# A context of 256 tokens is loaded in 32 by 32 blocks and turned by VectorE instead of TensorE

## Chip, core and metric

One core of one Trainium2 chip runs the whole kernel in one launch. The metric is the device time in microseconds (us) of that core. The median of three runs before the change is 1671.52 us (1669.97 to 1673.87).

## What is computed

Two blocks follow one another. The first one is two layers of attention (windowed heads and low-rank heads) on 256 tokens of 2048 features. The second one is two mixers on the same tokens, the first of which also needs states made from a context of 256 tokens. All of it is f32. What matters here is how the context enters:

```
# ctx: (1, 256, 2048); sh_c, sc_c come from a modulation of c_ctx, one value a feature
sh_c, sc_c = modulation(c_c, w_ada[i], b_ada[i], 2)
uc = ctx_s * (1.0 + sc_c) + sh_c
s_f, s_b = context_states(uc @ w_in_e[j][:, :E_STATE_COLS], w_gate_f[j], ...)
y, _, _ = even_mixer(u @ w_in_e[j], s_f, s_b, ...)
```

## The kernel before

All weights come from DRAM as one stream of 504 blocks ("slots") of 128 partitions by 1024 values, 512 KB each. SyncE issues them into a ring of 4 tiles `stage` (`load_slot`, line 636); the load of slot n waits until VectorE has split slot n-4. Each slot is split into a high and a low part, since TensorE multiplies in the rounded type fp32r: ScalarE copies `stage` to `wh` (`split_hi`, line 313, called as `hi()`), VectorE subtracts to get `wl` (`split_lo`, line 335, called as `lo()`). These parts have a ring of 4 of their own: `hi()` of slot n waits until TensorE is done with slot n-4. TensorE then does 12 products of 512 columns for the slot (`slot`, lines 396, 397 and 403). Each of ScalarE, VectorE and TensorE runs an order written out by hand, in which other work stands between slots at a fixed slot count n; nothing is planned by a program.

The activations must lie with features on the partitions (`xth` high part, `xtl` low part, 16 feature tiles of 256 tokens). For that, tiles with tokens on the partitions are turned in "turns": a turn is four transpositions of 128 by 128 on TensorE into one of two PSUM banks `TP` (`turn_in`, line 527), then ScalarE and VectorE read the bank (`turn_hi`, line 540, `turn_lo`, line 558). All turns are numbered in `TURNS`, and the bank of a turn is free once its reader has counted it.

The context goes this way in eight turns ("x", 2, m), m = 0 to 7. At the end of the second attention layer ScalarE issues one DMA of 2 MB into `arena` (line 964), when the last head is done. In the layer's last 16 slots, which are the second half of its output projection (named OUTB+0 to OUTB+15 here), TensorE does turns 0 to 3 after slots 6, 10, 14 and 15. The other four stand in front of the first four of the 32 slots of the context's own projection ("context slots"; lines 2470 to 2482). For each turn ScalarE multiplies and adds the modulation columns (`mcols`) in two instructions out of PSUM into the tile `Tb` in SBUF (line 548) and rounds it into `xth` (line 556), and VectorE makes `xtl` (line 568). Context slot m waits for turn m.

Beside this VectorE adds up the modulation of the second block (`mod_op`, line 696, on 512 KB blocks that GpSimd loads, three in flight), at most one instruction a slot, and adds the output projection to `X` (`evac_add`, line 1494). In the context slots, at n = 10, both engines take the statistics of the first block's last norm (`stats_act_sum`, `stats_act_root`, `stats_dve`, lines 614 to 631), at n = 11 and 12 VectorE scales `X` (line 1656), and from n = 28 the latent tokens are turned for the next projections (turn by turn, line 2482, with VectorE's part in line 1677).

Of the kernel before, what the change touches and what calls it, by code (L numbers as in the profile page):

```python
# [13 lines left out]
F32 = mybir.dt.float32  # L14
# [5 lines left out]
P = 128  # L20
# [61 lines left out]
    return t + [("m", l, 1, 1, 0), ("m", l, 1, 1, 1), ("x", l + 1, 2), ("x", l + 1, 3)]  # L82


TURNS = [t for l in range(DEPTH) for t in layer_turns(l)] + [("x", DEPTH, m) for m in range(4, 8)]
TURN = {name: n + 1 for n, name in enumerate(TURNS)}
HIGHS = [t for t in TURNS if t[0] in ("x", "lat", "ya", "yb")]
HIGH = {name: n + 1 for n, name in enumerate(HIGHS)}
# [31 lines left out]
def build(nc, A, out):  # L120
    ctx = ExitStack()
    with ctx:
# [447 lines left out]
        def kts(x, a, n=2):  # L570

            return x[:, a:a + n, :]
# [73 lines left out]
        def weight_of(p):  # L646
# [9 lines left out]
            half, g, m = (p - OUTA) // 16, (p - OUTA) % 16 // 4, p % 4  # L656
            return OUTA + 8 * g + 4 * half + m

        @block.sync
        def _(sp):  # L660
            x = A["x"][0].rearrange("(t p) n -> p t n", p=P)
            for l in range(DEPTH):
                for p in range(N_LAYER):
                    if l == 0 and p == 0:
                        sp.dma_start(X[:, :, 0:256], x[:, :, 0:256]).then_inc(once("x_first"), 16)
                    if l == 0 and 1 <= p < 5:
                        cs = slice(256 if p == 1 else COLS * (p - 1), COLS * p)
                        sp.dma_start(X[:, :, cs], x[:, :, cs]).then_inc(x_loaded[p - 1], 16)
                    if p == 16:
                        sp.wait_ge(st_sum, 2 * l + 1)  # L670
                        sp.dma_start(tail, A["w_tail"][l, :, :]).then_inc(tail_full, 16)
                    n = N_LAYER * l + p
                    load_slot(sp, n, N_LAYER * l + weight_of(p), n % SLOTS)
            with sp.Fori(R_BLOCK1, R_LAT0) as r:
                load_round(sp, r, r)
            with sp.Fori(R_LAT0, R_ODD0) as r:
                load_round(sp, r - R_KV, r)
            load_round(sp, R_ODD0 - R_KV + ODD_ORDER[0], R_ODD0)
            with sp.Fori(R_ODD0 + 1, R_ODD0 + 5) as r:
                load_round(sp, r - R_KV - 1, r)  # L680
            with sp.Fori(R_ODD0 + 5, R_END) as r:
                load_round(sp, r - R_KV, r)
            o = out[0].rearrange("(t p) n -> p t n", p=P)
            for i, (t, a, w) in enumerate(OUT_PIECES):
                sp.wait_ge(once("out_ready"), i + 1)
                sp.dma_start(o[:, t, a:a + w], X[:, t, a:a + w]).then_inc(out_done, 16)
            sp.wait_ge(out_done, 16 * len(OUT_PIECES))
# [100 lines left out]
        def _(act):  # L788
# [19 lines left out]
            def turn(name, dst, scale=None, bias=None):  # L808
                turn_hi(act, link, TURN[name], dst, scale, bias)

            def turn_x(l, m):
                if l < DEPTH:
                    turn(("x", l, m), kts(xth, 2 * m), [gcols[:, l, 2 * m + j:2 * m + j + 1] for j in range(2)])
                    return
                if m in (0, 4):
                    act.wait_ge(mod_cols, 4 if m == 0 else 8)
                turn(("x", l, m), kts(xth, 2 * m), [mcols[:, 0, KT + 2 * m + j:KT + 2 * m + j + 1] for j in range(2)],
                     [mcols[:, 0, 2 * m + j:2 * m + j + 1] for j in range(2)])

            def attention_layer(l):  # L820
                N0, G0, H0, e0 = N_LAYER * l, G_LAYER * l, HEADS * l, 2 * l
# [136 lines left out]
                for n in range(18):  # L958
                    hi()
                    if n == 0:  # L960
                        turn(("yb", l, 3), kts(xth, 14))
                    if n == 2 and l == DEPTH - 1:
                        act.wait_ge(o_done, HEADS * DEPTH)
                        act.dma_start(ar(8192, TT, D), A["ctx"][0].rearrange("(t p) n -> p t n", p=P))\
                            .then_inc(once("ctx_loaded"), 16)
                        act.dma_start(pa[:, 1024:1536], A["w_r"]).then_inc(once("wr_loaded"), 16)
                    if n in (8, 12, 16, 17):
                        turn_x(l + 1, (8, 12, 16, 17).index(n))

            for l in range(DEPTH):  # L970
                attention_layer(l)
# [390 lines left out]
        def _(dve):  # L1362
# [13 lines left out]
                turn_lo(dve, TURN[name], HIGH[name], hi, low, scaled, scale)  # L1376

            def turn_x(l, m):
                scale = [gcols[:, l, 2 * m + j:2 * m + j + 1] for j in range(2)] if l < DEPTH else None
                turn(("x", l, m), kts(xth, 2 * m), kts(xtl, 2 * m), l == DEPTH, scale)  # L1380

            def turn_lat(l, i):
                a, n = LAT_KT[i]
# [18 lines left out]
            def attention_layer(l):  # L1402
# [193 lines left out]
                for n in range(18):  # L1596
                    lo()
                    if n == 0:
                        turn(("yb", l, 3), kts(xth, 14), kts(xtl, 14), False)
                    if n in (8, 12, 16, 17):  # L1600
                        turn_x(l + 1, (8, 12, 16, 17).index(n))
                    if n in (10, 14):
                        mod_unit(1, (n - 10) // 4)
                    if n in (5, 9, 13, 17):
                        evac_add(1, (n - 5) // 4)
                    if n < 5:
                        mod()
# [38 lines left out]

            for n in range(4, 36):
                if n < 8:
                    turn_x(DEPTH, n)
                if n == 10:  # L1650
                    stats_dve(dve, e, [(0, 2, D)], ss, rstd, EPS)
                if n in (11, 12):
                    t = n - 11
                    dve.wait_ge(st_rs, e + 1)
                    dve.wait_ge(once("row_loaded"), 16)
                    nc.vector.scalar_tensor_tensor(out=X[:, t, :], in0=X[:, t, :], scalar=rstd[:, t:t + 1],
                                                   in1=ar(12288, D), op0=ALU.mult, op1=ALU.mult)\
                        .then_inc(once("x_final"), 1)
                lo()
                if n == 12:  # L1660
                    dve.wait_ge(once("wr_hi"), 1)
                    nc.vector.tensor_tensor(wr[:, :, 32:64], pa[:, 1024:1536].rearrange("p (a b) -> p a b", a=KT),
                                            wr[:, :, 0:32].bitcast(F32), ALU.subtract).then_inc(once("wr_ready"), 1)
                    for a in (0, P):
                        nc.vector.tensor_copy(rt_split[96:GK, a:a + P], ones[96:GK, :])
                if n == 23:
                    low_rank_sum(1)
                if n == 28:
                    gates_to_rows(1)
                if 24 <= n < 28:  # L1670
                    c = n - 24
                    dve.wait_ge(once("gate_hi"), c + 1)
                    low = gate_split[c][64:97, :]
                    nc.vector.tensor_tensor(low, gate_full[64:97, 512 * c:512 * c + 512], low.bitcast(F32), ALU.subtract)\
                        .then_inc(once("gate_lo"), 1)
                if n >= 28:
                    turn_scaled(n - 28)
                mod_ctx(n - 4)
# [501 lines left out]
        def _(pe):  # L2180
# [27 lines left out]
                    last = nc.tensor.matmul(AB[1][:, 392 + j:393 + j], macc[:, 0, P * j:P * j + P], ones[:, 0:1], start=True, stop=True)  # L2208
                last.then_inc(mod_summed, 1)

            ctx_tile = ar(8192, TT, D)
            Y = PROJ[:, :, 2048:4096]

            def turn(name, srcs):
# [5 lines left out]
            def turn_x(l, m):  # L2220
                if l == 0:
                    pe.wait_ge(x_loaded[m // 2] if m else once("x_first"), 16)
                elif l == DEPTH:
                    pe.wait_ge(once("ctx_loaded"), 16)
                else:
                    pe.wait_ge(psum_free, G_LAYER * (l - 1) + G_OUTB + m // 2 + 1 + 2)
                turn_rows(("x", l, m), ctx_tile if l == DEPTH else X, 2 * m)

            def attention_layer(l):
                N0, G0, H0 = N_LAYER * l, G_LAYER * l, HEADS * l  # L2230
# [201 lines left out]
                for n in range(16):  # L2432
                    step(OUTB + n)
                    if n == 0:
                        pe.wait_ge(o_done, H0 + HEADS)
                        turn_rows(("yb", l, 3), Y, 14)
                    if n in (8, 12):
                        turn_unit(1, (n - 8) // 4)
                    if n in (6, 10, 14, 15):
                        turn_x(l + 1, (6, 10, 14, 15).index(n))  # L2440
            for l in range(DEPTH):
                attention_layer(l)
# [26 lines left out]

            for p in range(4 * SLOTS):  # L2470
                g, m = p // SLOTS, p % SLOTS
                if p < 4:
                    turn_x(DEPTH, 4 + p)
                if g == 0:
                    turned(pe, TURN["x", DEPTH, m])
                slot(pe, 8 * R_CTX0 + p, G_BLOCK1 + g, KPB * m, m == 0)
                if p == 15:
                    low_rank(1)
                if g == 3:
                    if m == 0:  # L2480
                        pe.wait_ge(once("x_final"), 2)
                    transposes(pe, u, [lambda t, kt=2 * m + j: X[:, t, kt * P:kt * P + P] for j in range(2)])
# [360 lines left out]
```

## Time and profile before

| | us |
|---|---|
| median of three runs | 1671.52 |
| lowest, highest | 1669.97, 1673.87 |
| the profiled execution | 1672.03 |
| its span, first to last instruction | 1670.2 |
| TensorE busy in it | 1643.7 |
| VectorE busy | 1343.9 |
| ScalarE busy | 899.7 |
| DMA, mean over the span | 233 GB/s |

TensorE is busy for 98% of the span, at a mean granted clock of 0.997. All times of day below count from the start of the span. The second attention layer ends and the context slots begin at about 706 us.

### The profile page before, as it was taken

The numbers are of one execution on the slowest core, as the hardware profiler recorded it, in microseconds if no ns is written. First come the engines' busy times: TensorE is split into PE (matmuls) and PEld (weight loads), VectorE is DVE, ScalarE is ACT, GpSimd is POOL, SyncE is SP. The second block draws the span as 40 slices with busy tenths as digits, with TensorE's granted clock in tenths as the row PEclk, the third lists the DMA queues.
The fourth block names the chain that finished last, engine by engine and source line by source line (L and its number), as shares of the span: only waits on it lengthen the run. The fifth ranks groups of instructions, "written<-read, shape, count | busy, mean of one in ns | idle before, by whom it ended". The sixth has DMA issues, their size and how long they took to land.

```text
span 1670.2 us, 23384 instructions
## 1 busy us (share of the span) xinstructions
PE 1643.7 (98%) x8638; PEld 1400.1 (84%) x8638; DVE 1343.9 (80%) x1772; ACT 899.7 (54%) x1348; POOL 157.4 (9%) x221
## 2 busy tenths in 40 slices
PE   9999999999999999999999999999999999999996
PEld 8888888888888888887877878888877879999985
DVE  6998778979987878787985788888876988867766
ACT  6447564445466654565853466666534374445532
POOL 1100000001100000011211110010101101110000
PEclk9999999999999999999999999999999999999998
DMA  9975555658855545789987964345859869887663
GB/s 328 323 251 176 176 166 164 207 193 292 289 172 173 187 145 182 270 284 331 358 282 235 295 226 136 130 138 182 317 185 341 311 217 293 275 269 261 240 203 111
DMA packets 113160, 388.86 MB, mean 233 GB/s; under 512 B 18252, under 2 KB 19164, under 8 KB 111676
## 3 DMA queue, kind: packets, MB, share of 16 engines
q1 hardware_dynamic: 74944, 268.99, 45.9%
q0 software_dynamic: 27824, 101.18, 19.8%
q10 hardware_dynamic: 10286, 17.25, 3.0%
q8 instruction: 69, 1.13, 0.3%
q14 instruction: 37, 0.30, 0.1%
HBM read 383.19 MB, written 4.19 MB: 232 GB/s over the span
## 4 chain that ended last, share of the span: by engine, by line
PE 93%; DVE 3%; DMA 2%; ACT 1%; issue 1%; DVEq 0%; ACTq 0%; SPq 0%
PE L L396 22%; PE L L397 22%; PE L L403 22%; PE L L442 4%; PE L L438 4%; PE L L436 4%; PE TP L534 3%; PE AB L2601 2%; PE AB L2301 1%; DMA stage<-in_w_stream 1%; PE TP L2314 1%; PE AB L2535 1%; PE AB L2617 1%; PE AB L2304 1%; PE AB L2327 1%
## 5 line engine op out<-in xcount | busy, mean ns | idle before, releaser
L317 ACT ACTIVATE wh<-stage 128x1024 fp32r<-128x1024 f32 x504 | 530.4, 1057 | 463.8 <-PE L L403 221.9
L338 DVE TENSOR_TENSOR wl<-stage,wh 128x1024 fp32r<-128x1024 f32 x504 | 612.8, 1221 | 203.3 <-ACT wh L317 201.8
L396 PE MATMUL L<-wh,xth 128*128 128x512 f32 (+1 forms) x1692 | 680.9, 402 | 1.9 <-DVE xtl L2026 1.3
L397 PE MATMUL L<-wh,xtl 128*128 128x512 f32 (+1 forms) x1692 | 659.0, 389 | 0.0
L403 PE MATMUL L<-wl,xth 128*128 128x512 f32 (+1 forms) x1692 | 454.0, 389 | 0.0
L396 PEld LDWEIGHTS L<-wh,xth 128*128 128x128 f32 x1692 | 318.2, 188 | 67.1 <-issue 3.2
L403 PEld LDWEIGHTS L<-wl,xth 128*128 128x128 f32 x1692 | 317.5, 188 | 66.4 <-DVE wl L338 1.0
L397 PEld LDWEIGHTS L<-wh,xtl 128*128 128x128 f32 x1692 | 318.5, 188 | 62.7 <-issue 2.4
L714 DVE SCALAR_TENSOR_TENSOR macc<-mstage,scols,macc 128x1024 f32<-128x1024 f32 x240 | 306.8, 1278 | 4.3 <-DMA mstage<-in_w_mod 3.8
L781 POOL DMA_DIRECT2D mstage<-in_w_mod x192 | 138.9, 724 | 1240.7 <-DVE macc L714 1044.5
L436 PE MATMUL L<-xth,wh 128*128 128x256 f32 x512 | 125.8, 284 | 0.0
L438 PE MATMUL L<-xtl,wh 128*128 128x256 f32 x512 | 125.6, 283 | 0.0
L438 PEld LDWEIGHTS L<-xtl,wh 128*128 128x128 f32 x512 | 98.4, 192 | 0.0
L436 PEld LDWEIGHTS L<-xth,wh 128*128 128x128 f32 x512 | 98.3, 192 | 0.0
L854 ACT ACTIVATE pa<-pa,st 128x128 f32<-128x128 f32 x96 | 43.0, 449 | 68.4 <-DVE st L1464 37.9
L442 PE MATMUL L<-xth,wl 128*128 128x256 f32 x512 | 71.9, 283 | 0.0
L442 PEld LDWEIGHTS L<-xth,wl 128*128 128x128 f32 x512 | 66.1, 192 | 0.0
L866 ACT ACTIVATE pa<-TP 128x384 f32<-128x384 f32 x48 | 23.5, 490 | 62.4 <-PE TP L2314 62.3
L534 PE MATMUL TP<-ident,arena 128*128 128x128 f32 x288 | 41.1, 273 | 3.7 <-ACT arena L980 2.3
L534 PEld LDWEIGHTS TP<-ident,arena 128*128 128x128 f32 x288 | 34.2, 141 | 10.9 <-issue 3.0
L1141 ACT ACTIVATE arena<-arena 128x256 f32<-128x256 f32 (+1 forms) x84 | 34.1, 464 | 16.8 <-DVE arena L1806 16.8
L1458 DVE SCALAR_TENSOR_TENSOR pa<-tab,AB 128x384 f32<-128x384 f32 x48 | 26.5, 552 | 19.3 <-PE AB L2305 16.3
(275 smaller groups left out, 1464.5 us busy)
## 6 DMA issues: line engine op xcount, KB each, us to landing
stage<-in_w_stream SPq DMA_DIRECT2D x504, 512.0 KB, 4.6
mstage<-in_w_mod POOLq DMA_DIRECT2D x192, 512.0 KB, 6.2
arena<-in_ctx ACTq DMA_DIRECT2D x1, 2048.0 KB, 9.2
x_kept<-X ACTq DMA_DIRECT2D x4, 512.0 KB, 10.3
X<-x_kept ACTq DMA_DIRECT2D x1, 2048.0 KB, 8.3
arena<-in_b_ada ACTq DMA_DIRECT2D x2, 1024.0 KB, 9.1
arena<-in_ln_g ACTq DMA_DIRECT2D x2, 1024.0 KB, 8.8
X<-in_x SPq DMA_DIRECT2D x3, 512.0 KB, 8.1
```

The costliest lines, as they stand in the source:

```text
L317: nc.scalar.activation(wh[:, s % SPLITS].rearrange("p a b -> p (a b)"), stage[:, s % RING, :], ACT.Copy).then_inc(hi_ready, 1)
L338: nc.vector.tensor_tensor(wl[:, s % SPLITS].rearrange("p a b -> p (a b)"), stage[:, s % RING, :], wh[:, s % SPLITS].rearrange("p a b -> p ...
L396: nc.tensor.matmul(dst[:, t, 0:width], xh, w, start=start and k == 0, stop=False, skip_group_check=True)
L397: nc.tensor.matmul(dst[:, t, 0:width], xl, w, start=False, stop=False, skip_group_check=True)
L403: last = nc.tensor.matmul(dst[:, t, 0:width], x[0][:, kt + k, t * P:t * P + P], wl[:, slot, k, 0:width], start=False, stop=True, skip_grou ...
L436: nc.tensor.matmul(o[:, j, :], w, xth[:, kt + k, :], start=start and k == 0 and j % 2 == 0, stop=False, skip_group_check=True)
L438: nc.tensor.matmul(o[:, j, :], w, xtl[:, kt + k, :], start=False, stop=False, skip_group_check=True)
L442: last = nc.tensor.matmul(o[:, j, :], wl[:, s, k, P * j:P * j + P], xth[:, kt + k, :], start=False, stop=True, skip_group_check=True)
L534: last = nc.tensor.transpose(bank[0:width, j, t * P:t * P + P], src(t), ident[:])
L714: nc.vector.scalar_tensor_tensor(out=acc, in0=block, scalar=col, in1=acc, op0=ALU.mult, op1=ALU.add).then_inc(mod_sum, 1)
L781: pool.dma_start(mstage[:, unit % MOD_UNITS, :].rearrange("p (c n) -> p c n", c=2), WM[n // KPB, :, 2 * cp:2 * cp + 2, COLS * k:COLS * k + ...
L854: ins = nc.scalar.activation(pr[b][:, a:a + w], pr[b][:, a:a + w], ACT.Exp, bias=ngm[:, 2 * b + t:2 * b + t + 1], scale=1.0 if swa else ML ...
```

## The change

The context comes into SBUF already cut in blocks of 32 by 32, so that what is left is a transposition inside each block, which VectorE can do. `ctx_rows(sp, b)` issues four DMAs for 32 tokens: the DMA for a puts columns 32a to 32a+31 of every feature tile on partitions 32a to 32a+31, where the partition is the token within its 32. One such DMA moves 64 KB in 512 pieces of 128 bytes. SyncE issues them behind the loads of slots OUTB+6 to OUTB+13, four after each, 32 in all; ScalarE's DMA of 2 MB goes away.

VectorE's `exchange_ctx(m)` turns the blocks of two feature tiles (128 by 512 values) into `Tb`; ScalarE then modulates in place, out of SBUF and not out of PSUM, and rounds; VectorE's `ctx_low(m)` makes the low part as before. The eight turns on TensorE, and their places in `TURNS`, are gone; context slot m waits for `ctx_low`. On ScalarE the first four come at n = 14, 15, 16, 17 of the layer's last 18 slots (before: 8, 12, 16, 17). On VectorE the exchange of m runs ahead of its low part: exchanges 0 and 1 at n = 14, then one exchange and one low part a slot.

```diff
+        ctx_blocks = ar(8192, KT, TOK)
+        def ctx_rows(sp, b):
+            sp.wait_ge(o_done, HEADS * DEPTH)
+            rows = A["ctx"][0, 32 * b:32 * b + 32, :].rearrange("j (k a i) -> a j k i", a=4, i=32)
+            for a in range(4):
+                sp.dma_start(ctx_blocks[32 * a:32 * a + 32, :, 32 * b:32 * b + 32], rows[a]).then_inc(once("ctx_loaded"), 16)
...
                     load_slot(sp, n, N_LAYER * l + weight_of(p), n % SLOTS)
+                    if l == DEPTH - 1 and OUTB + 6 <= p < OUTB + 14:
+                        ctx_rows(sp, p - OUTB - 6)
...
-                turn(("x", l, m), kts(xth, 2 * m), [mcols[:, 0, KT + 2 * m + j:KT + 2 * m + j + 1] for j in range(2)],
-                     [mcols[:, 0, 2 * m + j:2 * m + j + 1] for j in range(2)])
+                T = Tb[m % 2]
+                act.wait_ge(once("ctx_turned"), m + 1)
+                for j in range(2):
+                    kt = 2 * m + j
+                    ins = nc.scalar.activation(T[:, j, :], T[:, j, :], ACT.Identity, scale=mcols[:, 0, KT + kt:KT + kt + 1],
+                                               bias=mcols[:, 0, kt:kt + 1])
+                link(ins)
+                nc.scalar.activation(kts(xth, 2 * m), T, ACT.Copy).then_inc(once("ctx_high"), 1)
...
-                        act.dma_start(ar(8192, TT, D), A["ctx"][0].rearrange("(t p) n -> p t n", p=P))\
-                            .then_inc(once("ctx_loaded"), 16)
...
+            def exchange_ctx(m):
+                if m == 0:
+                    dve.wait_ge(once("ctx_loaded"), 16 * 32)
+                if m >= 2:
+                    dve.wait_ge(once("ctx_low"), m - 1)
+                nc.vector.transpose(Tb[m % 2].rearrange("p a b -> p (a b)"),
+                                    kts(ctx_blocks, 2 * m).rearrange("p a b -> p (a b)")).then_inc(once("ctx_turned"), 1)
+            def ctx_low(m):
+                dve.wait_ge(once("ctx_high"), m + 1)
+                nc.vector.tensor_tensor(kts(xtl, 2 * m), Tb[m % 2], kts(xth, 2 * m).bitcast(F32), ALU.subtract)\
+                    .then_inc(once("ctx_low"), 1)
...
+                    if l == DEPTH - 1 and n >= 14:
+                        if n == 14:
+                            exchange_ctx(0)
+                            exchange_ctx(1)
+                        else:
+                            ctx_low(n - 15)
+                            exchange_ctx(n - 13)
...
                 if n < 8:
-                    turn_x(DEPTH, n)
+                    if n == 4:
+                        ctx_low(3)
+                    if n < 7:
+                        exchange_ctx(n + 1)
+                    ctx_low(n)
...
-                if p < 4:
-                    turn_x(DEPTH, 4 + p)
                 if g == 0:
-                    turned(pe, TURN["x", DEPTH, m])
+                    pe.wait_ge(once("ctx_low"), m + 1)
```

## Rows read from the trace of the kernel before

**Rows 1.** The page's part 1: busy us (share of the span) xinstructions.

```profile
PE 1643.7 (98%) x8638; PEld 1400.1 (84%) x8638; DVE 1343.9 (80%) x1772; ACT 899.7 (54%) x1348; POOL 157.4 (9%) x221
```

**Rows 2.** Waits of TensorE over the span: us in total, times, longest.

```profile
PE TP L534 <- DVE xtl L568: 5.0, 3, 3.5
```

**Rows 3.** Chain of waits, 640 to 830 us, TensorE's part: start us, us, what.

```profile
674.58 0.91 PE L L403 x4
...
692.74 0.91 PE L L403 x4
695.46 0.91 PE L L403 x4
...
701.80 0.92 PE L L403 x4
702.71 0.44 PE TP L534 x4
705.00 0.91 PE L L403 x4
...
708.79 0.91 PE L L403 x4
...
711.99 0.92 PE L L403 x4
```

**Rows 4.** The same chain, 735 to 791 us.

```profile
735.73 1.07 ACT wh L317
...
750.81 8.99 DMA stage<-in_w_stream
...
762.31 13.56 DMA stage<-in_w_stream
...
789.65 0.70 DVE xtl L568
790.40 0.66 PE TP L534 x4
```

**Rows 5.** VectorE's groups by line, 685 to 730 us: busy us, mean ns.

```profile
L338 DVE TENSOR_TENSOR wl<-stage,wh 128x1024 fp32r<-128x1024 f32 x14 | 17.2, 1225 | 9.0 <-ACT wh L317 8.9
L714 DVE SCALAR_TENSOR_TENSOR macc<-mstage,scols,macc 128x1024 f32<-128x1024 f32 x4 | 5.1, 1278 | 0.0
L568 DVE TENSOR_TENSOR xtl<-pa,xth 128x512 fp32r<-128x512 f32 x7 | 4.8, 689 | 1.3 <-ACT xth L556 1.3
...
L711 DVE TENSOR_SCALAR macc<-mstage,scols 128x1024 f32<-128x1024 f32 x1 | 0.7, 748 | 0.0
```

**Rows 6.** VectorE in order of time, 728 to 765 us.

```profile
731.24 0.17 DVE L631 RECIPROCAL st<-st 128x2 f32<-128x2 f32 x1 [1.34 <-ACT st L623]
732.19 1.23 DVE L338 TENSOR_TENSOR wl<-stage,wh 128x1024 fp32r<-128x1024 f32 x1 [0.78 <-ACT wh L317]
```

**Rows 7.** Stretches: us; PE, PEld, DVE, ACT, POOL busy; PEclk, DMA share, GB/s.

```profile
665.00:670.00 5.00, 5.00 (x24) 4.14 (x23) 5.00 (x5) 0.76 (x1) 0.82 (x2) 1.00 1.00 415
...
663.00:685.00 22.00, 22.00 (x104) 18.30 (x104) 19.81 (x21) 11.00 (x13) 2.17 (x3) 1.00 0.99 378
...
690.00:710.00 20.00, 20.00 (x103) 16.49 (x103) 12.77 (x17) 12.11 (x18) 0.00 (x0) 1.00 0.54 172
...
1366.50:1367.00 0.50, 0.50 (x3) 0.39 (x3) 0.10 (x1) 0.50 (x2) 0.00 (x0) 1.00 0.56 4
1367.00:1367.50 0.50, 0.50 (x4) 0.36 (x3) 0.00 (x0) 0.50 (x2) 0.00 (x0) 1.00 0.96 7
1367.50:1368.00 0.50, 0.50 (x6) 0.50 (x5) 0.00 (x0) 0.50 (x1) 0.00 (x0) 1.00 0.53 4
```

**Rows 8.** ScalarE's two DMAs of 4-byte pieces, line 1095: issue ns, start, landing.

```profile
L1095 ACTq DMA_DIRECT2D lcols<-in_ln_b x1: 2280/2280/2280, 920.4 to 920.4; - x1
...
DMA to landing us min/median/max: 5.8/6.9/8.0
```

**Rows 9.** ScalarE in order of time, 655 to 740 us.

```profile
671.92 1.06 ACT L317 ACTIVATE wh<-stage 128x1024 fp32r<-128x1024 f32 x1 [6.16 <-DMA stage<-in_w_stream]
```

More of the change, by code:

```diff
@@ L82, in layer_turns @@
     return t + [("m", l, 1, 1, 0), ("m", l, 1, 1, 1), ("x", l + 1, 2), ("x", l + 1, 3)]
-TURNS = [t for l in range(DEPTH) for t in layer_turns(l)] + [("x", DEPTH, m) for m in range(4, 8)]
+TURNS = [t for l in range(DEPTH) for t in layer_turns(l) if t[0:2] != ("x", DEPTH)]
 TURN = {name: n + 1 for n, name in enumerate(TURNS)}
@@ L963, in attention_layer @@
                         act.wait_ge(o_done, HEADS * DEPTH)
-                        act.dma_start(ar(8192, TT, D), A["ctx"][0].rearrange("(t p) n -> p t n", p=P))\
-                            .then_inc(once("ctx_loaded"), 16)
                         act.dma_start(pa[:, 1024:1536], A["w_r"]).then_inc(once("wr_loaded"), 16)
-                    if n in (8, 12, 16, 17):
-                        turn_x(l + 1, (8, 12, 16, 17).index(n))
+                    places = (14, 15, 16, 17) if l == DEPTH - 1 else (8, 12, 16, 17)
+                    if n in places:
+                        turn_x(l + 1, places.index(n))
             for l in range(DEPTH):
@@ L1378, in turn_x @@
             def turn_x(l, m):
-                scale = [gcols[:, l, 2 * m + j:2 * m + j + 1] for j in range(2)] if l < DEPTH else None
-                turn(("x", l, m), kts(xth, 2 * m), kts(xtl, 2 * m), l == DEPTH, scale)
+                turn(("x", l, m), kts(xth, 2 * m), kts(xtl, 2 * m), False, [gcols[:, l, 2 * m + j:2 * m + j + 1] for j in range(2)])
+            def exchange_ctx(m):
[9 more added lines that the diff above has]
+                    .then_inc(once("ctx_low"), 1)
             def turn_lat(l, i):
@@ L1599, in attention_layer @@
                         turn(("yb", l, 3), kts(xth, 14), kts(xtl, 14), False)
-                    if n in (8, 12, 16, 17):
+                    if l < DEPTH - 1 and n in (8, 12, 16, 17):
                         turn_x(l + 1, (8, 12, 16, 17).index(n))
+                    if l == DEPTH - 1 and n >= 14:
[5 more added lines that the diff above has]
+                            exchange_ctx(n - 13)
                     if n in (10, 14):
@@ L2209, in odd_columns @@
                 last.then_inc(mod_summed, 1)
-            ctx_tile = ar(8192, TT, D)
             Y = PROJ[:, :, 2048:4096]
@@ L2222, in turn_x @@
                     pe.wait_ge(x_loaded[m // 2] if m else once("x_first"), 16)
-                elif l == DEPTH:
-                    pe.wait_ge(once("ctx_loaded"), 16)
                 else:
                     pe.wait_ge(psum_free, G_LAYER * (l - 1) + G_OUTB + m // 2 + 1 + 2)
-                turn_rows(("x", l, m), ctx_tile if l == DEPTH else X, 2 * m)
+                turn_rows(("x", l, m), X, 2 * m)
             def attention_layer(l):
@@ L2438, in attention_layer @@
                         turn_unit(1, (n - 8) // 4)
-                    if n in (6, 10, 14, 15):
+                    if l < DEPTH - 1 and n in (6, 10, 14, 15):
                         turn_x(l + 1, (6, 10, 14, 15).index(n))
```

## The prediction

> **What bounds the kernel now.** I read the busy times first: TensorE is busy for 98% of the span, VectorE for 80% [rows 1]. Then TensorE's waits: it waits little, and its longest waits are for VectorE's low part of a turn, 5.0 us in three, one of them 3.5 us [rows 2]. Then I followed the chain of waits through the stretch that the change touches. Up to about 735 us it is TensorE alone, slot after slot: products, turns, products [rows 3]. There the reader should see that a turn costs its own time on the path. Behind that it changes: from 735.73 to 790.40 us the chain goes through ScalarE, VectorE, two weight transfers of 8.99 and 13.56 us and VectorE again, and it gets back to TensorE at 790.40, at a transposition that has waited 3.5 us [rows 2, 4]. So the eight turns are on the path locally, while a barrier some 75 us later is set by VectorE and the DMA queues. What the change brings is what arrives at that barrier, not what TensorE saves in front of it.
>
> **What TensorE saves.** The low products of two slots with nothing between them start 2.72 us apart (692.74 and 695.46). With one turn between it is 3.20 us (701.80 to 705.00, 708.79 to 711.99), although the turn's own piece is 0.44: the next slot begins more slowly. With two turns, m = 3 and 4, it is 3.79 us (705.00 to 708.79) [rows 3]. So one turn is 0.48 and the pair 1.07; six single ones and the pair make 6 x 0.48 + 1.07 = 3.95 us. All of it falls before 718 us. TensorE also gets new waits, for `ctx_low`; they are walked through below.
>
> **What VectorE pays.** Eight transpositions of 128 by 512 are added; the subtractions stay. The trace has no transposition on VectorE. The nearest rows: a two-input subtraction of 128 by 512 is 0.69 us, one of 128 by 1024 is 1.23, a one-input TENSOR_SCALAR of 128 by 1024 is 0.75 [rows 5]. From below half of the last is 0.37; from above I put twice the 0.69, about 1.3, in case a block is filled and emptied one after the other. I take 0.69, of which the next instruction overlaps about 0.08 (neighbours in time start that much before the end), so 0.61 each and 4.9 us in all. The Trainium skill, "Vector Engine (DVE) Microarchitecture Reference", in what it says of the transpose mode, has it pipelined at one element a cycle and lane. No row shows one; by that rule 512 elements would cost like the subtraction of the same width, and the upper end would not occur.
>
> Cover: in 685 to 730 us VectorE idled 9.0 us in front of its splits, waiting for ScalarE, plus 1.3 [rows 5]. But part of this goes too, since TensorE's slots now end sooner. So I walked the three engines in order of time from 697 us, with 2.72 us a slot, 1.06 and 1.23 for a split's two halves, 1.6 for ScalarE's part of a turn, 0.69 for a low part and 1.28 for a modulation step. Exchange 0 can start at 697.9, behind the split of n = 14. ScalarE waits there for it with the next split queued behind, so this split comes some 2 us late; the split ring is three slots ahead (8.2 us), and TensorE doesn't feel it. Low parts 0 to 3 are ready 1.4 to 1.7 us before context slots 0 to 3 want them, the last ones 1.2 us before. So TensorE doesn't stall there, by a small margin. On VectorE an iteration with an exchange, a low part, a split and a modulation step is 0.61 + 0.61 + 1.14 + 1.19 = 3.55 us against 2.72 of a slot; it falls behind and arrives at the statistics (n = 10) with a split of its own just done. Before, the split behind the statistics began at 732.19 [rows 6]; in the walk it begins at 730.3. VectorE is then busy without a break to 749 us, where the weight load of the chain is issued [rows 4]. So the barrier comes 1.9 us earlier, and TensorE, which is there 3.95 us earlier, waits 3.5 + 3.95 - 1.9 = 5.6 us instead of 3.5. With 0.3 a transposition the walk gives 3.4 us, with 0.9 it gives 0.2, with 1.2 a loss of 1.9 and TensorE itself stalls for 4.2 us.
>
> **What the DMA pays.** One transfer of 2 MB becomes 32 of 64 KB with 16,384 pieces of 128 bytes. At full share the engines move 415 GB/s, so the bytes are 2.10 MB / 415 = 5.1 us in both forms [rows 7]. For the pieces: the 2048 four-byte pieces of the pool scale's load around 1367 us took 0.5 x (0.56 + 0.96 + 0.53) = 1.02 us of all engines' time, that is 0.5 ns a piece and 8.2 us for 16,384 [rows 7]. Beside other traffic the two loads of line 1095 landed at 920.0 + 5.8 and 920.4 + 8.0, so 2048 pieces took 2.6 us, which would be 21 us for all [rows 8]. From below nothing is added. I take 8.2, so 13.3 us in place of 5.1. Before, the queues were full from 663 to 685 us (0.99) and half idle from 690 to 710 (0.54) [rows 7]; 8.2 us more fill them to about 700.
>
> Who waits for that: the weights, which share SyncE's queue. Four issues per slot are added on SyncE, and the second load of line 1095 held its issuer for 2.28 us [rows 8]; even so they fit in a slot. Before, the load of OUTB+6 stood beside the 2 MB, and its split could start only at 671.92, after 6.16 us of waiting [rows 9]; TensorE wanted it at 674.58 + 0.91 = 675.5 [rows 3], so 2.5 us of margin were left after the split's 1.06. Now this load goes ahead of the first pieces and gains several us. From then on a slot needs 1.3 us for its weights (0.52 MB / 415), 1.7 for pieces and 0.6 for modulation (half a block), 3.6 us against 2.72, over eight slots 7 us of a lead of about 12 (four `stage` tiles). I book nothing. The eighth group lands near 692, before exchange 0 at 697.9. All else (semaphore renumbering, ScalarE reading SBUF in place of PSUM, SyncE's satisfied wait for the last head) hides behind TensorE's slots: nothing, and up to 0.2 us each where a margin is that small.
>
> **The sum.** Profiled execution: 1672.0 - 3.95 (turns) + 2.05 (longer wait at 790 us) = 1670.1. Its time lies 0.5 over the median, so for the median 1671.5 - 1.9 = 1669.6 us. A run of this kernel is told from no change from about 0.2%, 3.3 us, on.
>
> **Rivals.** (a) The gain arrives whole. If the stretch from 735 to 790 us moves with TensorE, because the transposition is nearer 0.3 or the weight transfers of 8.99 and 13.56 us shrink once VectorE issues sooner, the result is 1671.5 - 3.95 = 1667.6. For it: ScalarE's split at 735.73, where the chain leaves TensorE, is released by TensorE [rows 4]. Against it: VectorE's own load grows by 4.9 us just there.
> (b) VectorE becomes the bound of the context slots: the transposition is 0.9 to 1.3. Then context slots wait for low parts and the barrier moves by +0 to +2: 1671.5 to 1673.5. For it: iterations of 3.55 us against 2.72; against it, all one-pass rows of this width at 0.69 or less [rows 5].
> (c) Slower: the pieces hold the weights back. The place is SyncE's queue at OUTB+7 to OUTB+13. It decides from about 1.1 ns a piece on: then a slot needs 1.3 + 2.3 + 0.6 = 4.2 us, and seven slots beyond 667 us end at 696, when TensorE wants OUTB+13. At the 2.6 us per 2048 of the busy row plus bytes, 3.3 us, a slot needs 5.2, the last one lands 7 to 9.5 us late, and with 3.95 saved the end is some 5.5 us later: 1677. For it: the busy row [rows 8]. Against it: the idle row, and that the busy one holds others' traffic as well. The Trainium skill, "DMA: Bandwidth & Descriptors", Specifications, says that pieces below 512 bytes don't reach the line rate and are done as read-modify-write; this speaks for (c), no row of mine shows such a read, and with the bytes counted twice the pieces would take 18.4 us, just at the point from which (c) decides.
>
> **How the numbers follow.** Forecast 0.48, (a) 0.24, (b) 0.10, (c) 0.18. The forecast's own spread, given a transposition between 0.45 and 0.8, is 1668.6 to 1671. Faster by over 0.2% is (a) and a little of the forecast's lower edge, 0.27; slower is (c) and the far end of (b), 0.21; the rest, 0.52, is no change. The range reaches into (a) and (c): 1666.8 to 1676.5.
>
> **What would show it.** TensorE: no transposition between 677 and 718 us, low products 2.72 us apart all through, no wait for `ctx_low`, and a wait of about 5.6 us near 788 us in place of 3.5; if that wait is still 3.5 or less, (a) holds. VectorE: a transposition of 0.69 us, the split behind the statistics at about 730.3. DMA: a share near 1 to about 700 us and no wait of TensorE for a high part. The forecast is wrong if context slots wait for VectorE, or if a product of OUTB+7 to OUTB+15 waits for a split whose load is late.

## The result: 0.35% slower, with the weights late behind the pieces

| | before | after |
|---|---|---|
| median, us | 1671.70 (7 runs) | 1678.48 (7 runs) |
| lowest, highest | 1669.88, 1673.87 | 1677.43, 1679.09 |
| profiled execution | 1672.03 | 1678.41 |
| its span | 1670.2 | 1676.6 |

The ratio on record is 1.0035, with a 95% interval of [1.0025, 1.0044]; it isn't the quotient of the two medians, which is 1.0041, and the two differ by up to 0.0006 in all that follows. The kernel became slower by more than the 0.2% that can be told from no change. 1678.5 lies outside the range of the prediction and nearest to rival (c), which gave 1677.

The busy line of the changed kernel, and the line of its DMA packets:

```profile
PE 1643.7 (98%) x8606; PEld 1400.4 (84%) x8606; DVE 1348.1 (80%) x1780; ACT 900.6 (54%) x1348; POOL 157.1 (9%) x221
DMA packets 129783, 388.85 MB, mean 232 GB/s; under 512 B 35132, under 2 KB 36044, under 8 KB 128556
```

Against [rows 1] TensorE has 32 instructions fewer and the same busy time; a part of that is that some now run at the lower clock (below). VectorE has 8 more and 4.2 us more. No busy time says why the kernel is slower; the waits of TensorE do (us in total, times, longest):

```profile
PE L L396 <- DVE xtl L1409: 5.1, 1, 5.1
PE TP L534 <- DVE xtl L568: 2.9, 3, 1.4
PE L L396 <- ACT wh L317: 2.7, 4, 0.9
```

Two of these are new: 5.1 us for the context's first low part, and 2.7 us in four waits for high parts of weights. The old wait at the barrier, 3.5 us [rows 2], shrank to 1.4. In order of time on TensorE (start, us, what, idle before it and its releaser):

```profile
686.10 0.50 PE L396 MATMUL L<-wh,xth 128*128 128x512 f32 x1 [0.89 <-ACT wh L317]
689.61 0.50 PE L396 MATMUL L<-wh,xth 128*128 128x512 f32 x1 [0.50 <-ACT wh L317]
693.42 0.50 PE L396 MATMUL L<-wh,xth 128*128 128x512 f32 x1 [0.80 <-ACT wh L317]
696.91 0.47 PE L396 MATMUL L<-wh,xth 128*128 128x512 f32 x1 [0.48 <-ACT wh L317]
...
714.03 0.79 PE L396 MATMUL L<-wh,xth 128*128 128x512 f32 x1 [5.05 <-DVE xtl L1409]
...
719.32 0.62 PE L396 MATMUL L<-wh,xth 128*128 128x512 f32 x1
...
722.31 0.39 PE L396 MATMUL L<-wh,xth 128*128 128x512 f32 x1
```

ScalarE tells why the high parts are late. Before, it waited once for 6.16 us and then caught up [rows 9]. Now it waits for every weight block:

```profile
675.04 1.06 ACT L317 ACTIVATE wh<-stage 128x1024 fp32r<-128x1024 f32 x1 [5.78 <-DMA stage<-in_w_stream]
679.61 1.06 ACT L317 ACTIVATE wh<-stage 128x1024 fp32r<-128x1024 f32 x1 [3.51 <-DMA stage<-in_w_stream]
684.99 1.06 ACT L317 ACTIVATE wh<-stage 128x1024 fp32r<-128x1024 f32 x1 [4.32 <-DMA stage<-in_w_stream]
688.50 1.06 ACT L317 ACTIVATE wh<-stage 128x1024 fp32r<-128x1024 f32 x1 [2.45 <-DMA stage<-in_w_stream]
```

These waits name a DMA, but most of the loads were issued late. SyncE in order of time (start, us; L666 is the context, L640 the weights):

```profile
672.74 1.79 SPq L640 DMA_DIRECT2D stage<-in_w_stream  x1
674.57 2.91 SPq L666 DMA_DIRECT2D arena<-in_ctx  x4
677.53 1.68 SPq L640 DMA_DIRECT2D stage<-in_w_stream  x1
679.25 3.53 SPq L666 DMA_DIRECT2D arena<-in_ctx  x4
682.83 1.65 SPq L640 DMA_DIRECT2D stage<-in_w_stream  x1
684.52 3.25 SPq L666 DMA_DIRECT2D arena<-in_ctx  x4
687.81 0.62 SPq L640 DMA_DIRECT2D stage<-in_w_stream  x1
688.47 2.57 SPq L666 DMA_DIRECT2D arena<-in_ctx  x4
```

The reader should see that there is no gap: each row starts within 0.1 us of the end of the one above. From 674.57 to 679.25, to 684.52, to 688.47 one round takes 4.68, 5.27 and 3.95 us, while TensorE uses up a slot every 2.72. All eight rounds, from the weight load at 663.85 to the one at 698.04, take 34.2 us in place of 21.8. A piece DMA is never under 0.565 us, and a weight load at times takes 1.79 (duration in ns, min/median/max):

```profile
L666 SPq DMA_DIRECT2D arena<-in_ctx x32: 565/627/2087, 664.2 to 697.4; - x32
...
L640 SPq DMA_DIRECT2D stage<-in_w_stream x19: 327/353/1791, 658.8 to 718.9; - x19
```

Of 663 to 700 us, 11 weight blocks were issued where the kernel before issued 15. Their time to landing hardly changed, a median of 5.2 against 5.1 us.

The DMA engines have little room either (columns as in [rows 7]):

```profile
663.00:685.00 22.00, 22.00 (x102) 18.24 (x101) 15.59 (x15) 6.31 (x8) 2.17 (x3) 1.00 0.97 229
685.00:710.00 25.00, 21.32 (x94) 16.27 (x92) 14.76 (x18) 9.04 (x10) 0.00 (x0) 1.00 0.93 254
```

The longest rounds, 4.8 to 5.6 us, lie between 667 and 688 us, where the share of 5 us stretches reaches 1.07 (the profile's share can come out above 1). The shortest group of four in the list takes 2.57 us and the shortest weight load 0.33, so without any lengthening a round would be 3.0 us, and eight of them would overrun their slots by 2 us and not by 12. That SyncE's queue is where the weights are held is shown. What lengthens an issue there, the work of issuing or engines that take no more, this trace can't tell apart.

The chain of waits from there to the barrier:

```profile
704.06 1.07 ACT wh L317
705.15 1.23 DVE wl L338
...
708.71 0.63 DVE pa L1403
...
709.42 1.10 ACT pa L832 x2
...
712.15 1.23 DVE wl L338
713.38 0.61 DVE xtl L1409
...
744.33 1.07 ACT wh L317
...
759.41 7.63 DMA stage<-in_w_stream
769.55 12.46 DMA stage<-in_w_stream
795.79 0.70 DVE xtl L568
796.54 0.66 PE TP L534 x4
```

The first exchange runs at 708.71 and not at 697.9, since VectorE comes to it only behind the late splits; and the last pieces, which were to land near 692, are issued until 697.99. Exchange, modulation and low part stand one after the other on two engines, a weight split is in the queue between them, and TensorE waits until 714.03. After that idle time the granted clock is at the lower level (same columns):

```profile
714.00:718.00 4.00, 3.97 (x9) 3.14 (x10) 3.75 (x5) 3.92 (x7) 0.00 (x0) 0.50 0.64 190
718.00:722.00 4.00, 4.00 (x15) 3.19 (x14) 3.93 (x7) 3.20 (x7) 0.00 (x0) 0.78 0.83 299
722.00:726.00 4.00, 4.00 (x20) 3.30 (x19) 4.00 (x6) 3.82 (x6) 0.72 (x1) 1.00 0.95 346
```

0.50 is 1.2 GHz, 1.00 is 2.4 GHz. The slot from 714.03 to 719.32 takes 5.29 us in place of 2.72, the next one 2.99.

**The account.** ScalarE's split where the chain leaves TensorE comes at 744.33 and not at 735.73 [rows 4], 8.60 us later. 0.70 of that is there before the first piece is issued (the low product at 640.09 us before stands at 640.78, the one at 671.69 at 672.39). The other 7.9 us: waits 2.7 + 5.05; the slow slot and the one behind it 2.57 + 0.27; the restart after each of the four small waits, 0.29 each (689.61 - 686.10 = 3.51 = 2.72 + 0.50 + 0.29), 1.2; less the turns, 3.95. Sum: 7.8. From there to the barrier it is 52.2 us against 54.7, so 2.5 us come back, and the barrier is 6.14 us later. The profiled execution is 6.4 us longer.

### The profile page after: what moved, and what is told of

Read it like the earlier page. It is cut to its first block, busy times and chain, and to the rows that moved or that the text cites. A ratio compares the mean times of both kernels' runs of the same rounds, so it can differ in the third digit from the quotient of the medians.

```text
span 1676.6 us, 23351 instructions
## 1 busy us (share of the span) xinstructions
PE 1643.7 (98%) x8606; PEld 1400.4 (84%) x8606; DVE 1348.1 (80%) x1780; ACT 900.6 (54%) x1348; POOL 157.1 (9%) x221
## 4 chain that ended last, share of the span: by engine, by line
PE 87%; DVE 5%; DMA 3%; ACT 2%; issue 1%; SPq 1%; ACTq 0%; DVEq 0%
PE L L396 20%; PE L L397 20%; PE L L403 20%; PE L L438 4%; PE L L442 4%; PE L L436 4%; DMA stage<-in_w_stream 3%; PE TP L534 2%; PE AB L2637 2%; DVE wl L338 2%; PE AB L2339 1%; DVE macc L725 1%; PE TP L2352 1%; ACT wh L317 1%; PE AB L2571 1%
## 5 line engine op out<-in xcount | busy, mean ns | idle before, releaser
L1519 DVE SCALAR_TENSOR_TENSOR arena<-AB,st,arena 128x64 f32<-128x64 f32 (+1 forms) x96 | 25.0, 302 | 19.5 <-PE AB L2365 18.3
L534 PE MATMUL TP<-ident,arena 128*128 128x128 f32 x256 | 36.3, 273 | 3.7 <-ACT arena L996 2.3
```

Source lines behind the costliest of these rows:

```text
L534: last = nc.tensor.transpose(bank[0:width, j, t * P:t * P + P], src(t), ident[:])
```

## Experiments

Two theories at first. **Issue**: four DMAs of 512 pieces a slot are more than SyncE can issue in time. **Engines**: the pieces take the DMA engines' time, whoever issues them. Ratios are to the kernel before, run on the same chip.

### One load again, VectorE still turns

```diff
-                    if l == DEPTH - 1 and OUTB + 6 <= p < OUTB + 14:
-                        ctx_rows(sp, p - OUTB - 6)
+                        act.dma_start(ar(8192, TT, D), A["ctx"][0]...).then_inc(once("ctx_loaded"), 16)
```

> The changed kernel with its 32 DMAs on SyncE taken out and the one DMA of 2 MB on ScalarE put back in its old place; VectorE's transpositions and all else stay (the blocks are then not where they should be, so the context's values are wrong; the work is the same). Theory P (the 16,384 pieces are the whole loss, wherever they cost it): no wait of TensorE for a high part in 683 to 700 us, no wait for ctx_low, the barrier near 790 us about 1.9 us earlier than before, time 1671.7 - 1.9 = 1669.8. Rival V (VectorE's eight transpositions at 0.61 are dearer for the context slots than I walked): TensorE waits for ctx_low or a low part there, time 1671 to 1673.

Measured: 1668.04 us (12 runs) against 1673.22, ratio 0.9972 [0.9963, 0.9981]: faster by 4.7 us. TensorE has no wait for `ctx_low`. VectorE's split behind the statistics, and the end of the chain:

```profile
728.79 1.23 DVE L338 TENSOR_TENSOR wl<-stage,wh 128x1024 fp32r<-128x1024 f32 x1 [0.79 <-ACT wh L317]
```

```profile
757.11 12.14 DMA stage<-in_w_stream
...
783.02 0.70 DVE xtl L568
783.77 0.66 PE TP L534 x4
```

The split that was to come at 730.3 comes at 728.79, and one long weight transfer is left in place of two [rows 4]. So the loss is in how the context comes in, and the trade between TensorE and VectorE is a gain, larger than predicted. The DMA engines in this form, for comparison with the changed kernel:

```profile
663.00:685.00 22.00, 22.00 (x103) 18.30 (x102) 18.70 (x19) 9.33 (x9) 2.17 (x3) 1.00 0.97 376
685.00:710.00 25.00, 25.00 (x116) 20.78 (x115) 20.53 (x29) 15.28 (x23) 0.00 (x0) 1.00 0.63 203
```

### No transposition at all

`exchange_ctx` does nothing and ScalarE reads the one load directly.

> One load of 2 MB as in e1, and VectorE's eight transpositions left out: ScalarE reads the context tile directly (values wrong). TensorE has no turns and VectorE nothing more than before. My walk says that the barrier near 790 us moves with VectorE, so without the transpositions nearly the whole 3.95 us of TensorE's saving should arrive: 3.4 to 3.9 us, time 1668.0. Rival: the stretch from 750 to 790 us is set by the DMA queues alone and doesn't move with what is issued a little earlier: then the gain is the same as in e1 or nothing, 1669.8 to 1671.7.

Measured: 1667.60 us (7 runs), ratio 0.9968 [0.9956, 0.9980]. The barrier is at 783.96. The two forms differ by 0.04%, and their intervals overlap, so no cost of the eight transpositions on VectorE can be told from nothing.

### Half of the issues on ScalarE

```diff
-            for a in range(4):
+            for a in parts:        # SyncE (0, 1); ScalarE (2, 3), at n = 4 to 11
```

> The changed kernel with the DMAs for a = 2 and 3 of each group issued by ScalarE, after its splits n = 4 to 11; a = 0 and 1 stay on SyncE. The pieces, their bytes and the engines' traffic are the same. Theory I (the issue on SyncE is what is slow, some 0.63 us for a DMA of 512 pieces, 1.2 ns a piece, one after the other): SyncE needs 2 x 0.63 + 0.4 = 1.7 us a slot in place of 3.3, the weights come in time, and the time falls to about 1670 to 1672. Rival E (the 16 engines are full with the pieces): the share of the DMA engines stays near 1 and the time stays at 1676 to 1679. Rival D (SyncE and ScalarE share what makes the pieces): issues of both get longer than 0.63 while the other issues, and the time stays at 1676 or more.

Measured: 1673.47 us (11 runs), ratio 1.0000 [0.9991, 1.0009]. Relieving SyncE gives back the whole 0.35% by which the change was slower, with the pieces, their number and their slots the same. So the engines' work on the pieces, which is the same here, doesn't make that loss alone. The time lies nearer to the theory of the issue (1670 to 1672) than to its rivals (1676 or more). How it comes back isn't shown: the one trace is of its slowest execution, 1679.96 us, 6.5 above the median. In it TensorE waits for no high part, but for the context as long as in the changed kernel. That wait, and the weight loads issued in 663 to 700 us:

```profile
PE L L396 <- DVE xtl L1411: 5.1, 1, 5.1
```

```profile
stage<-in_w_stream SPq DMA_DIRECT2D x12, 512.0 KB, 8.4
```

12 blocks are issued, one more than in the changed kernel, a weight load takes up to 3.13 us to issue, and the blocks land after 8.4 us in the median in place of 5.2, with a DMA share of 1.03 in 663 to 685 us.

### Sixteen slots in place of eight

```diff
-                sp.dma_start(ctx_blocks[32 * a:32 * a + 32, :, 32 * b:32 * b + 32], rows[a])...
+                sp.dma_start(ctx_blocks[32 * a:32 * a + 32, 8 * h:8 * h + 8, 32 * b:32 * b + 32],
+                             rows[a][:, 8 * h:8 * h + 8])...
```

> The changed kernel with the same 16,384 pieces of 128 bytes on SyncE, but cut in two halves of the features and so in 64 DMAs of 256 pieces: the first 32 (feature tiles 0 to 7) behind the loads of OUTB+6 to OUTB+13 as before, the other 32 behind the next eight loads (OUTB+14, OUTB+15 and the first six context slots). VectorE waits for the first half before exchange 0 and for the second before exchange 4. Two pieces of the price are halved per slot: the issue on SyncE and the engines' time. Theory P (a slot needs more than 2.72 us only because all pieces stand in eight slots): SyncE needs 4 x 0.35 to 4 x 0.45 + 0.4 = 1.8 to 2.2 us a slot, the engines 1.27 + 0.87 + 0.6 = 2.7; no wait of TensorE for a high part and none of 5 us for ctx_low; time near the one with one load, 1668 to 1670. Rival: the issue has a fixed part of 0.4 us or more a DMA beside full engines, and 64 of them hold the weights as much as 32 did: 1674 to 1679.

Measured: 1672.89 us (11 runs), ratio 0.9999 [0.9990, 1.0008], between what the two theories gave. Half the pieces a DMA doesn't take half the time to issue:

```profile
L669 SPq DMA_DIRECT2D arena<-in_ctx x64: 430/451/1448, 663.0 to 706.9; - x64
```

A round of SyncE is about 2.45 us from 687 us on, under a slot; before that it is up to 3.85. A form of it in which VectorE turns the first two blocks two slots earlier followed:

> As e5, and VectorE's exchanges 0 and 1 at n = 12 and 13 (not 14), its low parts 0 and 1 at n = 13 and 15, ScalarE's parts at n = 12, 14, 16, 17. VectorE then has more air in the context slots. If the order in e5 already hides VectorE's part, the time is that of e5 within 0.1%; if the narrow margins of 1.2 to 1.7 us cost there, it is 1 to 2 us faster. If the first half of the context hasn't landed at n = 12 (about 692 us), VectorE stalls with its splits behind it and the time is 1 to 3 us slower.

Measured: 1672.09 us (12 runs), ratio 0.9995 [0.9985, 1.0005]. It is within 0.1% of the form above, so the order on VectorE is not what is left.

### Long pieces on 32 partitions, middle ones on 128

Both keep 32 DMAs of 64 KB from SyncE, four a slot.

```diff
+  32 partitions x 2048 bytes:  ar(8192, 4096)[32 * a:32 * a + 32, 512 * b:512 * b + 512]
+ 128 partitions x  512 bytes:  ar(8192, 4096)[:, 512 * b + 128 * a:512 * b + 128 * a + 128]
```

> The changed kernel with each of the 32 DMAs made of 32 pieces of 2048 bytes in place of 512 of 128 (other parts of the context land in the same bytes, so values are wrong; bytes, count of DMAs, queue and places are the same). Theory P: time as with one load, 1669.8. If it is the number of DMAs and not of pieces that costs (32 issues of at least 0.33 us plus a fixed part each): SyncE still needs 5 x 0.35 to 5 x 0.6 us a slot and the time is 1672 or more.

> As e3 (32 DMAs of 64 KB on SyncE in the changed kernel's places, values wrong), but each DMA over all 128 partitions with one piece of 512 bytes on each, in place of 32 partitions with one piece of 2048. e3 was 4 us above the one load although its pieces are long, with weight loads landing after 7.6 us (median) and the engines at a share of 1.00 while moving 299 GB/s. Theory W (a DMA onto 32 partitions only is slow for all that share the queues): weight loads land after about 5 us again and the time falls to about 1668 to 1669. Rival F (it is the 32 issues of 0.42 us on SyncE): SyncE's issues take as long, and the time stays at 1672.

Measured: long pieces on 32 partitions 1672.15 us (12 runs), ratio 0.9994 [0.9984, 1.0004]; 512 bytes on 128 partitions 1669.41 us (12 runs), ratio 0.9976 [0.9967, 0.9985]. Their issues cost the same:

```profile
L666 SPq DMA_DIRECT2D arena<-in_ctx x32: 421/422/739, 663.2 to 684.1; - x32
...
DMA to landing us min/median/max: 3.2/7.6/9.5
```

```profile
L666 SPq DMA_DIRECT2D arena<-in_ctx x32: 429/433/1748, 663.0 to 685.9; - x32
...
DMA to landing us min/median/max: 3.0/4.8/6.6
```

The first fence is the long pieces: four times fewer of them, and yet they land later, and 663 to 685 us moves 299 GB/s at share 1.00 against 315 at 0.97. Weight blocks issued in 663 to 700 us land after 7.6 against 5.9 us. The second form comes out close to what theory W gave (1668 to 1669), and the cost of the issue alone, the same in both, isn't what separates them. The traces don't show where the long pieces lose their 0.18%: the profiled execution with long pieces, 1667.78 us, is the fastest of its runs, and the other one, 1670.68, is slower than its median.

### Both issuers and sixteen slots; half the pieces

> The two remedies together: 64 DMAs of 256 pieces of 128 bytes (two halves of the features), of which SyncE issues those for a = 0, 1 (two a slot, in 16 slots) and ScalarE those for a = 2, 3 (two a slot at n = 4 to 11, four a slot at n = 12 to 15). The result stays the reference's. Theory A (what e2_half_on_act and e5_sixteen_slots, both at the time before, still lack against e1_one_load is the time that the 16,384 pieces take of the DMA engines, some 11 us more than one load, beside a stretch where weights lead by little): neither issuer is the bound already in e5, so nothing more is gained, ratio to before 0.999 to 1.001, and weight landings in 663 to 700 us stay near 5 us or rise. Rival B (the rest is SyncE's issue time, 1.9 to 2.6 us a slot in e5 that delays each weight load behind it): with one half of it gone the ratio falls toward that of e1_one_load, 0.9972: 0.9980 or less.

Measured: 1671.11 us (11 runs) against 1672.48, ratio 0.9988 [0.9978, 0.9997], between what the two theories gave. 15 weight blocks are issued in 663 to 700 us, as many as before the change, and land after 7.2 us. Here SyncE has gaps: a weight load and two DMAs take 1.3 us of a slot, and the DMA share is 1.02 in 663 to 685 us and 1.00 in 685 to 710. So what is left is no longer SyncE's issue. It is the best form that puts the whole context where it belongs, and its gain is less than what can be told from no change.

> Only the first half of the features comes as pieces (8192 of 128 bytes in 32 DMAs of 256, four a slot behind OUTB+6 to OUTB+13); the second half comes as one plain DMA of 1 MB from ScalarE, where the kernel before had its 2 MB, and VectorE turns it like the others, so that half of the context's values is wrong. SyncE's rate of issue per slot is that of e5_sixteen_slots, in 8 slots in place of 16. Theory A (the cost that is left goes with the number of pieces): half of the way from e5 (0.9999) to e1_one_load (0.9972), ratio about 0.9985, 2.4 us faster than before. Rival B (it goes with the rate of issue in the slots whose weights are latest): as in e5, 0.9995 to 1.0003. Rival C (the first half costs nothing since the lead of the weights covers it, only the second half of the pieces is late): as in e1, 0.9972 to 0.9978.

Measured: 1669.18 us (11 runs), ratio 0.9980 [0.9971, 0.9989]. B is excluded; A (0.9985) and C's band (0.9972 to 0.9978) are both in the interval. Half of the blocks costs about a third of the distance from one load (0.9972) to the sixteen slots (0.9999).

### The same pieces on 128 partitions

The first changes only where the 256 pieces of a DMA go; the second puts the whole context where it belongs.

```diff
-            for a in range(4): ... ctx_blocks[32 * a:32 * a + 32, 8 * h:8 * h + 8, 32 * b:32 * b + 32]
+            for a in range(4): ... ctx_blocks[:, 8 * h + 2 * a:8 * h + 2 * a + 2, 32 * b:32 * b + 32]
...
+            for k in (8 * h + 2 * q, 8 * h + 2 * q + 1): ... ctx_blocks[:, k, 32 * b:32 * b + 32], rows[:, :, k]
```

> e5_sixteen_slots with one thing changed: each of its 64 DMAs still moves 256 pieces of 128 bytes from SyncE, four a slot, but puts two on each of 128 partitions in place of eight on each of 32 (other values of the context, so its states are wrong). What is left between e5 (0.9999) and e1_one_load (0.9972) is the question. Theory A (it is the number of pieces): nothing changes, ratio 0.9992 to 1.0003, DMA share and GB/s in 663 to 685 us as in e5 (1.02, 287). Rival B (it is that a DMA goes onto 32 partitions alone: long pieces on 32 partitions, e3, gave 0.9994, and short ones on 128, e8, gave 0.9976): the ratio falls to 0.9972 to 0.9982, and the stretch 663 to 685 us moves 310 GB/s or more.

> A form with the reference's result and no DMA on 32 partitions: one feature tile and 32 tokens a DMA, 128 DMAs of 128 pieces of 128 bytes, one on each of 128 partitions. Half are issued by SyncE (four a slot in 16 slots), half by ScalarE (four a slot at n = 4 to 11, eight a slot at n = 12 to 15). e9_sixteen_both_issuers is the form to compare it with (0.9988). If rival B of e11 holds (32 partitions are the cost): 0.9972 to 0.9982, the first form that keeps most of the gain. If the pieces are the cost: 0.9985 to 0.9995. If the issue is (128 DMAs of at least 0.33 us, four of them and a weight load 1.7 us a slot on SyncE, eight a slot 2.7 us on ScalarE): ScalarE's splits come late at n = 12 to 15, TensorE waits for high parts there, 1.0000 or more.

Measured: the first 1672.03 us (12 runs) against 1673.71, ratio 0.9993 [0.9982, 1.0004], with 273 GB/s at share 0.95 in 663 to 685 us. The ratio lies in A's band, the interval only touches the edge of B's, and the stretch is far from B's 310 GB/s: short pieces cost on 128 partitions too. The second: 1692.88 us (4 runs), ratio 1.0119 [1.0098, 1.0140], over three times the loss of the change. I had put its issue at 0.33 us; it is 0.53 to 1.45, on SyncE and, below, on ScalarE:

```profile
699.98 5.51 ACTq L670 DMA_DIRECT2D arena<-in_ctx  x8
705.59 1.06 ACT L317 ACTIVATE wh<-stage 128x1024 fp32r<-128x1024 f32 x1 [4.57 <-issue]
705.62 6.60 ACTq L670 DMA_DIRECT2D arena<-in_ctx  x8
712.32 1.06 ACT L317 ACTIVATE wh<-stage 128x1024 fp32r<-128x1024 f32 x1 [5.67 <-issue]
```

TensorE waits 13.2 us for low parts of the context, once for 11.7 us. In 685 to 710 us the DMA share is only 0.64: the engines have room, and what is slow is the issue, on both queues; on ScalarE it holds up the splits as well. This is the plainest sign of it in the study, by a miss of mine.

## Why the prediction was wrong

**Right.** The transpositions are gone from TensorE and its slots are 2.72 us apart where nothing waits. The price on VectorE, taken as 0.69 us:

```profile
L1403 DVE STREAM_TRANSPOSE pa<-arena 128x512 f32<-128x512 f32 x8 | 5.5, 703 | 0.1
```

The Trainium skill, "Vector Engine (DVE) Microarchitecture Reference", says of the transpose mode that it sustains one element a cycle and lane. The trace agrees with what I took from it, that a transposition costs like a subtraction of the same width: 703 ns against 689 [rows 5].

**The engines' time** for the pieces was booked too low. Share times length of 663 to 710 us is 0.97 x 22 + 0.63 x 25 = 37.1 us with one load, and 0.97 x 22 + 0.93 x 25 = 44.6 us in the changed kernel, which moved 2.0 MB less in it (4.7 us at 415 GB/s). So the pieces took some 12 us more than one load, an estimate, where 8.2 were booked. With the 5.1 us of the bytes that is 17.3 us, 2.2 us a slot or 1.1 ns a piece. Rival (c) was to decide from 2.3 us a slot on, bytes included, so by the prediction's own sum the engines stood just short of it: 1.3 + 2.2 + 0.6 = 4.1 us a slot and not 3.6.

**The step that failed** is "Four issues per slot are added on SyncE [...] even so they fit in a slot" and "I book nothing". I had a row that spoke against it, the issue of 2.28 us [rows 8], and dismissed it without a sum. With the shortest times measured a round is 3.0 us, already over a slot of 2.72; the eight rounds were 3.3 to 5.6 us and ran 12.4 us over their slots. That is the whole lead of about 12: weights 2.7 us late, the context 5.05, and the clock 2.8 more. That ScalarE as a second issuer gives back 0.35% shows that the queue of SyncE is the place, and the 128-DMA form does the reverse. How much of the 12.4 us is issuing as such, and how much is lengthened by engines with a share near 1, stays open.

**Rival (c)** had the place (SyncE's queue, OUTB+7 to OUTB+13) and nearly the time, 1677, which the stated range of up to 1676.5 left out. Its cause, a price per piece on the engines, isn't the whole: the layout costs 0.63% (1.0035 against 0.9972), and with half of the issues on ScalarE and the same pieces 0.35 of it comes back, 0.28 doesn't. The Trainium skill, "DMA: Bandwidth & Descriptors", Specifications, spoke for (c) with its rule for pieces below 512 bytes. In size the runs agree with its direction: 512-byte pieces on 128 partitions were 0.24% faster than the kernel before, 128-byte ones 0.07%, although spread over twice as many slots. That a read stands behind it no trace here shows.

**The barrier step** was too pessimistic by its own terms. It was to come 1.9 us earlier; with one load it comes 6.2 us earlier (measured from the low product near 671.5 us), 3.0 of it at the split behind the statistics (60.5 us behind that product before, 57.5 now), the rest behind it, where the chain has one full weight transfer in place of two. TensorE's wait at the barrier is 1.1 us, where I had 5.6 and (a) had 3.5 or less. So without the pieces rival (a) is what happens: 4.7 us against the 3.95 it allowed. That it is more than TensorE saves goes with the shorter chain. Of the 6.6 us by which the barrier is earlier in the profiled execution, 4.65 arrive at its end: behind it stand one wait of 1.0 us that the kernel before doesn't have, and a granted clock of 0.98 in 900 to 1000 us in place of 1.00. I had argued against (a) with VectorE's 4.9 us; with one load VectorE was busy for 20.5 us of the 25 from 685 to 710 us, 17.0 before, with room left.

**Open.** Between the sixteen-slot form (0.9999) and one load (0.9972) lie 4.5 us. Short pieces on 128 partitions (0.9993) and long pieces on 32 (0.9994) each lose most of that alone, middle ones on 128 (0.9976) don't. From one load to sixteen slots the DMA share in 685 to 710 us rises from 0.63 to 0.96, which speaks for engine time as a part of it; how it divides between length and partitions, and why 32 partitions cost, isn't settled.

## What to carry to other kernels

Count the issue time of a DMA like an instruction of its queue, behind which all later loads stand: what a queue issues slot after slot has to fit in a slot, with more room for it where the DMA engines are full. A wait "for a DMA" can be a wait for its issue, which the order of the issuing queue shows at once by the missing gaps. And try a change's two halves apart: here the compute half was a gain of 0.28%, which the layout half more than used up.

## What the runs showed of the hardware

Issue time on SyncE depends on the shape, not on bytes alone: 0.33 us for 512 KB in 128 rows, 0.42 for 32 pieces of 2 KB, 0.43 for 128 of 512 bytes, 0.43 to 0.45 for 256 of 128 bytes, 0.565 to 0.63 for 512 of them. It isn't the number of pieces alone either: 128 pieces of 128 bytes, whose source has one dimension more than that of the 128 pieces of 512, took 0.53 at least and 0.68 in the median. These are least times and medians; single ones took up to 2.09 us, and behind such DMAs even a plain weight load took up to 1.79 us in the changed kernel, where the kernel before had 0.35 at most in the same stretch. DMAs that ScalarE issues hold up its own work: eight of them took 5.5 us, and the split behind them waited 4.6. Pieces of 128 bytes took the 16 engines some 0.7 ns each beyond the same bytes in one load, an estimate from the shares above. After 5.05 us without work TensorE ran its next slot at 1.2 GHz, 5.29 us in place of 2.72; after waits of 0.9 us or less the granted clock stayed at 1.00 (663 to 710 us) and a restart cost 0.29 us.
